# Forget logits with the tokens moving, two modulation pairs moved past a score bias, compressed products in another order

## The reference, cut to what matters

```python
# token mix of the first block: compressed attention, per head; 15 compressed keys
s_c = einsum('bghqd,bgnd->bghqn', qb, k_c) * scale - slope * d_c
p_c = masked_softmax(s_c, cmp_end <= t)
o_c = einsum('bghqn,bgnd->bghqd', p_c, v_c)

# hybrid layer
mod = silu(c) @ w_ada + b_ada              # 6 x 1024 values
h = modulate_2(x, norm1_w, shift1, scale1)
x_in, conv_b, conv_c, q, k, v, f_logit, gate_conv_l, gate_attn_l = split(h @ w_in)
log_f = log_sigmoid(f_logit + b_forget)    # 8 heads
F = cumsum(log_f)                          # along the tokens
s = q_i @ k.T * scale + (F_i[:, None] - F[None, :])
y_b = softmax(causal(s)) @ v               # q and k normed per head
merged = sigmoid(gate_conv_l) * p_a + sigmoid(gate_attn_l) * p_b
x = x + gate1 * (merged @ w_o)
```

## Time and profile before

| what | us |
|---|---|
| median of 3 runs | 1853.35 (1852.48 to 1854.16) |
| profiled execution, its own time | 1855.78 |
| its span, first to last instruction | 1854.1 |
| TensorE busy (matmul) in the span | 1764.3 (95%) |
| VectorE, ScalarE busy | 1376.3 (74%), 957.9 (52%) |
| mean granted TensorE clock, share of full | 0.978 |

### The profile page before, as it was taken

One profiled execution on the slowest core, in us unless ns is written; L12 is line 12 of the kernel. 1 busy time (PEld: TensorE's weight loads), 2 busy tenths in 40 slices (PEclk: granted clock), 3 DMA queues, 4 the chain that ended last, 5 costly groups with the idle time before them and its releaser, 6 DMA issues.

```text
span 1854.1 us, 24899 instructions
## 1 busy us (share of the span) xinstructions
PE 1764.3 (95%) x8645; PEld 1427.1 (77%) x8645; DVE 1376.3 (74%) x2097; ACT 957.9 (52%) x1433; POOL 46.9 (3%) x92
## 2 busy tenths in 40 slices
PE   5999999999999999999999999999899897999998
PEld 3788778787788878886878777887687775888876
DVE  6887676766876578777677578775776477999997
ACT  3444354664544454445437554444434546777775
POOL 0000000000000000000000000000000000000000
PEclk8999999999999999999989999999998998999999
DMA  8988743134576758884612338986562533999994
GB/s 361 359 324 301 287 172 136 69 127 169 204 280 257 255 187 336 316 305 174 248 69 92 135 138 311 343 302 245 189 253 93 203 136 114 363 347 375 347 350 166
DMA packets 61802, 437.43 MB, mean 236 GB/s; under 512 B 6816, under 2 KB 7328, under 8 KB 9504
## 3 DMA queue, kind: packets, MB, share of 16 engines
q1 hardware_dynamic: 47504, 339.27, 48.6%
q0 software_dynamic: 12672, 92.28, 13.4%
q10 hardware_dynamic: 1552, 4.89, 0.8%
HBM read 435.36 MB, written 1.05 MB: 235 GB/s over the span
## 4 chain that ended last, share of the span: by engine, by line
PE 82%; DVE 11%; ACT 4%; issue 2%; DMA 1%; ACTq 0%; SPq 0%; DVEq 0%; POOLq 0%
PE bank L1754 24%; PE bank L1755 24%; PE bank L1756 24%; DVE w_lo L945 2%; PE bank L1977 2%; DVE ada_w L969 1%; ACT w_hi L506 1%; PE bank L1995 1%; DMA ada_w<-ada_pairs 1%; PE bank L1836 1%; PE bank L1957 1%; DVE arena L1243 1%; PE bank L2005 1%; PE bank L1955 1%; PE bank L2297 1%
## 5 line engine op out<-in xcount | busy, mean ns | idle before, releaser
L945 DVE TENSOR_TENSOR w_lo<-raw,w_hi 128x1024 fp32r<-128x1024 f32 x426 | 501.5, 1220 | 223.2 <-ACT w_hi L506 222.9
L506 ACT ACTIVATE w_hi<-raw 128x1024 fp32r<-128x1024 f32 x426 | 426.5, 1053 | 363.3 <-PE bank L1756 359.2
L1754 PE MATMUL bank<-w_hi,uT_hi 128*128 128x512 f32 (+3 forms) x1424 | 558.4, 392 | 20.3 <-DVE uT_lo L1260 12.6
L1755 PE MATMUL bank<-w_lo,uT_hi 128*128 128x512 f32 (+3 forms) x1424 | 543.9, 382 | 0.0
L1756 PE MATMUL bank<-w_hi,uT_lo 128*128 128x512 f32 (+3 forms) x1424 | 543.4, 382 | 0.0
L1754 PEld LDWEIGHTS bank<-w_hi,uT_hi 128*128 128x128 f32 x1424 | 271.5, 191 | 80.1 <-DVE uT_lo L1260 14.0
L1756 PEld LDWEIGHTS bank<-w_hi,uT_lo 128*128 128x128 f32 x1424 | 270.7, 190 | 52.1
L1755 PEld LDWEIGHTS bank<-w_lo,uT_hi 128*128 128x128 f32 x1424 | 271.6, 191 | 48.6 <-issue 1.4
L1754 PE MATMUL bank<-w_hi,r_arena 128*128 128x512 f32 (+1 forms) x744 | 299.1, 402 | 6.2 <-DVE r_arena L1652 2.3
L1755 PE MATMUL bank<-w_lo,r_arena 128*128 128x512 f32 (+1 forms) x744 | 295.1, 397 | 0.0
L1756 PE MATMUL bank<-w_hi,r_arena 128*128 128x512 f32 (+1 forms) x744 | 292.6, 393 | 0.0
(11 more groups left out here) (328 smaller groups left out, 1470.6 us busy)
## 6 DMA issues: line engine op xcount, KB each, us to landing
raw<-weight_stream SPq DMA_DIRECT2D x216, 1024.0 KB, 4.9
ada_w<-ada_pairs POOLq DMA_DIRECT2D x88, 1024.0 KB, 5.2
raw<-expert_blocks SPq DMA_DIRECT2D x48, 1024.0 KB, 4.8
ada_w<-expert_blocks SPq DMA_DIRECT2D x32, 1024.0 KB, 4.9
cmpw<-expert_blocks SPq DMA_DIRECT2D x16, 1024.0 KB, 4.8
arena<-ada_pairs SPq DMA_DIRECT2D x5, 1024.0 KB, 13.8
ada_w<-ada_pairs SPq DMA_DIRECT2D x3, 1024.0 KB, 13.8
cmpw<-compress_w ACTq DMA_DIRECT2D x2, 1024.0 KB, 8.7
```

The costliest lines, as they stand in the source:

```text
L506: act.activation(w_hi[:, b], v, ACT.Copy).then_inc(hi_done, 1)
L945: V.tensor_tensor(w_lo[:, b], v, f32(w_hi[:, b]), ALU.subtract).then_inc(split_done, 1)
L1754: pe.matmul(dst, xh, w_hi[:, off:off + n], start=first, stop=False, skip_group_check=True)
L1755: pe.matmul(dst, xh, w_lo[:, off:off + n], start=False, stop=False, skip_group_check=True)
```

## The change

Three parts. The forget products hold 8 weight columns stationary and move 256 tokens, 24 products into 8 rows; ScalarE copies these to `f_lT`, TensorE turns them back between the two halves of gate set 0, and the copy to `f_row` waits for that. The last two of the late pairs leave the fourth unit; ScalarE copies `c_next` to `c_kept` (the second half of `cmpw`), and VectorE does the pairs from there, behind the first job's bias; VectorE's wait for all pairs ahead of the q and k norms goes. The compressed products run over the row groups in the innermost loop.

```diff
--- before.py
+++ after.py
@@ -218,6 +218,7 @@
         qkv = at(4096, T, HYB_QKV)
         gates_h = at(7168, T, 2 * D)
         gate_sets_h = [gates_h[:, :, i * 512:(i + 1) * 512] for i in range(4)]
+        f_lT = at(8704, T, P, parts=8)
         f_row = at(11264, T, 8)
         f_e, f_l, f_cum = at(11280, T, 8), at(11296, T, 8), at(11312, T, 8)
         nlogf = at(11392, T, P)
@@ -369,7 +370,8 @@
                 return (1, b + (13 + i // 2), g0 + (24 + i)) if i % 2 == 0 else (0, a + (13 + i // 2), g0 + (24 + i))
             return 1, b + (i + 13), g0 + (i + 26)
 
-        LATE_PAIRS = [(0, 1), (2, 3), (4, 5), (6, 7)]
+        LATE_PAIRS = [(0, 1), (2, 3), (4, 5), ()]
+        c_kept = cmpw[:, 1, 1024:2048]
 
         def late_pair(i):
 
@@ -778,10 +780,13 @@
                 split(u + m + 1, (2,))
 
             act.wait_ge(w_done, DEPTH * 7 + 5)
+            act.activation(f_lT[:, :, :], SPARE[0:8, 128:128 + S].rearrange("p (t s) -> p t s", t=T), ACT.Copy).then_inc(rT_ready, 1)
+            split(u + 5, (0,))
+            act.wait_ge(r_psum, 1)
             act.activation(f_row[:, :, :], SPARE[:, 0:16].rearrange("p (t h) -> p t h", t=T), ACT.Copy).then_inc(w_evac_a, 1)
-            split(u + 5, (0,))
             act.wait_ge(qkn_ms, 1)
             act.activation(qk_ss, qk_ss, ACT.Sqrt).then_inc(qkn_sq, 1)
+            act.activation(c_kept, c_next, ACT.Copy).then_inc(c_ready, 1)
 
             act.wait_ge(exp_in, 1)
             act.activation(f_e[:, :, :], f_e[:, :, :], ACT.Exp).then_inc(exp_out, 1)
@@ -796,6 +801,7 @@
                 act.wait_ge(q_psum, DEPTH * 2 + b + 1)
                 act.activation(qT_h[:, 2 * b:2 * b + 2], bank[2 + 4 * b][:, :].rearrange("p (c s) -> p c s", c=2), ACT.Copy,
                                scale=qk_gain[:, 0:1]).then_inc(q_ready, 1)
+            act.wait_ge(c_ready, 2 * DEPTH + 2)
             for b in range(2):
                 act.wait_ge(kh_psum, b + 1)
                 act.activation(kT_h[:, 2 * b:2 * b + 2], bank[4 + b][:, :].rearrange("p (c s) -> p c s", c=2), ACT.Copy,
@@ -1221,8 +1227,9 @@
                         e = V.tensor_tensor(ov[:, a], ov[:, a], tv[:, a], ALU.add)
                     link(e)
 
-            def jobs_run(j0, jobs, beside=lambda j: None):
+            def jobs_run(j0, jobs, beside=lambda j: None, first=lambda: None):
                 job_bias(j0, jobs, 0)
+                first()
                 for j, (kind, qt, g) in enumerate(jobs):
                     if j + 1 < len(jobs):
                         job_bias(j0, jobs, j + 1)
@@ -1500,7 +1507,6 @@
             link(V.tensor_tensor(f_row[:, :, :], f_row[:, :, :], bf, ALU.add))
             V.tensor_scalar(f_cum[:, :, :], f_row[:, :, :], 0.0, None, ALU.min)
             V.scalar_tensor_tensor(f_e[:, :, :], f_row[:, :, :], -1.0, f_row[:, :, :], ALU.mult, ALU.min).then_inc(exp_in, 1)
-            dve.wait_ge(ada_done, STAGES * PAIRS)
             dve.wait_ge(qkn_sq, 1)
             link(V.reciprocal(qk_ss, qk_ss))
             for i in range(2):
@@ -1552,7 +1558,12 @@
                 if j >= 2:
                     split(um, (j - 2,))
 
-            jobs_run(DEPTH * NJ, HYB_JOBS, hyb_beside)
+            def last_pairs():
+                dve.wait_ge(c_ready, 2 * DEPTH + 2)
+                for j in (6, 7):
+                    ada_pair(late_pair(j), mods[:, 72 + 2 * j:74 + 2 * j], c_kept)
+
+            jobs_run(DEPTH * NJ, HYB_JOBS, hyb_beside, first=last_pairs)
 
             def last_modulation():
                 dve.wait_ge(ada_done, STAGES * PAIRS)
@@ -1589,7 +1600,7 @@
                 V.tensor_tensor(xn_lo[:, t], xn[:, t], f32(xn_hi[:, t]), ALU.subtract).then_inc(xn_ready, 1)
             expert_split(0, 0, (0, 1), IN_LINE)
 
-            dve.wait_ge(r_psum, 1)
+            dve.wait_ge(r_psum, 2)
             link(V.tensor_copy(logits[:, :, :], GU[1][:, 128:256].rearrange("p (t c) -> p t c", t=T)[:, :, 0:36]))
             lg = logits[:, :, 0:4]
 
@@ -2106,10 +2117,10 @@
                 up(1, bank[3], 0, uk_psum)
                 up(0, bank[0], 1024, uv_psum)
                 pe.wait_ge(kvc_ready, l + 1)
-                for p in range(2):
-                    half = slice(DH * p, DH * p + DH)
-                    for qt in range(2):
-                        for i in range(4):
+                for qt in range(2):
+                    for i in range(4):
+                        for p in range(2):
+                            half = slice(DH * p, DH * p + DH)
                             m = pe.matmul(bank[4 + p][:, 64 * qt + 16 * i:64 * qt + 16 * i + N_CMP], qT[half, i, tok(qt)], kT_cmp[half, i // 2, 0:N_CMP],
                                           start=True, stop=True, skip_group_check=True)
                 m.then_inc(cs_psum, 1)
@@ -2129,10 +2140,10 @@
                     for i in range(2):
                         m = turn_rows(bank[Q_BANKS[b]][:, i * S:i * S + S], lambda t, h: q_tok[:, t, h], 2 * b + i, QK)
                     m.then_inc(qm_psum, 1)
-                for i in range(4):
-                    rows = slice(32 * i, 32 * i + N_CMP)
-                    for qt in range(2):
-                        for p in range(2):
+                for qt in range(2):
+                    for p in range(2):
+                        for i in range(4):
+                            rows = slice(32 * i, 32 * i + N_CMP)
                             m = pe.matmul(bank[CO_BANKS[i]][:, 128 * qt + 64 * p:128 * qt + 64 * p + 64], pT_cmp[rows, 2 * p + qt], v_cmp[rows, i // 2],
                                           start=True, stop=True, skip_group_check=True)
                 m.then_inc(co_psum, 1)
@@ -2193,8 +2204,9 @@
             seen = {m: set() for m in (4, 5, 6)}
             for k in range(KD):
                 need(u + 4, seen[4], 8 * k, 8)
-                for t in range(T):
-                    m = mm3(SPARE[:, 8 * t:8 * t + 8], uT_hi[:, k, tok(t)], uT_lo[:, k, tok(t)], 8 * k, 8, k == 0 and t == 0, k == KD - 1)
+                for w, v in ((w_hi, uT_hi), (w_lo, uT_hi), (w_hi, uT_lo)):
+                    m = pe.matmul(SPARE[0:8, 128:128 + S], w[:, 8 * k:8 * k + 8], v[:, k], start=k == 0 and w is w_hi and v is uT_hi,
+                                  stop=k == KD - 1 and v is uT_lo, skip_group_check=True)
             m.then_inc(used[0], 1)
             release(w_done)
 
@@ -2209,7 +2221,12 @@
 
             pe.wait_ge(w_evac_a, DEPTH * 9 + 6)
             pe.wait_ge(w_evac_v, DEPTH * 3 + 3)
-            hyb_gates(0)
+            hyb_gates(0, range(4))
+            pe.wait_ge(rT_ready, 1)
+            for t in range(T):
+                m = pe.transpose(SPARE[:, 8 * t:8 * t + 8], f_lT[:, t], ident[0:8, 0:8])
+            m.then_inc(r_psum, 1)
+            hyb_gates(0, range(4, KD))
             pe.wait_ge(logf_ready, 1)
             pe.matmul(SPARE[:, 0:8], tri[:, 0:P], nlogf[:, 0, 0:8], start=True, stop=True, skip_group_check=True)
             pe.matmul(SPARE[:, 8:16], ones, nlogf[:, 0, 0:8], start=True, stop=False, skip_group_check=True)
@@ -2276,7 +2293,7 @@
                                   stop=k == KD - 1 and v is uT_lo, skip_group_check=True)
             m.then_inc(rT_psum, 1)
             release(used[2])
-            pe.wait_ge(rT_ready, 1)
+            pe.wait_ge(rT_ready, 2)
             for t in range(T):
                 m = pe.transpose(GU[1][:, 128 + 64 * t:128 + 64 * t + 36], logits_T[:, t], ident[0:36, 0:36])
             m.then_inc(r_psum, 1)
```

## The result

The changed kernel takes 1840.82 us (median of 10 runs, 1836.00 to 1846.99). The kernel before, run beside it, takes 1852.25 (10 runs, 1848.82 to 1854.56). The ratio is 0.9942, with a 95% interval of 0.9931 to 0.9953: 11.4 us or 0.6% faster. The profiled execution of the changed kernel took 1841.11 us.

What follows compares the result with a forecast made beforehand. TensorE's own sequence and the handoffs it waits for were taken to bound the kernel. Hybrid stretch 3.4 plus layers 1.7 made 5.1 us off the 1853.35 median: 1848.2 us, range 1844.8 to 1851.6.

Steps and rivals of the forecast that it cites:

- The forget products: Hybrid layer: new products save 3.9 us, gate set 0 at full clock 1.9; TensorE reaches the sums 5.5 earlier.
- ScalarE as the next late thing: Hybrid layer: ScalarE's in-order chain delays q's copy, so the first scores come 4.1 us earlier, not 5.5.
- The pairs: Two late pairs, 4.6 us on VectorE, fit its later 9.34 us pause free; the hybrid gain needs their move.
- Queues: SP's expert loads, behind its stream, and POOL's pair loads are not delayed by the later pairs: nothing.
- The clock in the hybrid stretch: Clock falls with the first hybrid scores; 0.7 us lost, so the hybrid term is 4.1 - 0.7 = 3.4.
- Compressed products: Both layers' compressed attention: 0.0625 us per instruction, scores 2.0 (1.3 saved), sums 2.0 (0.5 saved).
- wide overlap rival: Compressed sums: alternated products run at 0.028 us each; 7.4 us saved in all, 1846.0; chance 0.16.
- The 0.8 for the first layer's scores: First layer: VectorE waited 0.78 us for the scores, so 0.8 of their saving counts on the path.
- Layers: Compressed attention in the first block's two layers: 0.5 us in the second plus 1.2 in the first, 1.7.
- No effect of alternation: Compressed products: each product's two passes keep one group, loads stay serial; 3.4 us alone, 1850.0; chance 0.12.
- drain at each change of group: Compressed products: 52 more row-group changes drain the array at 0.16 us each, 8.3 us; slower, 1858.2; chance 0.08.
- Clock: Hybrid layer: fall comes with the first scores, 3.4 us further into set 1; hybrid 0.9, total 2.6, 1850.7; chance 0.17.

Runs made afterwards that it cites:

- e5: Changed kernel with the two late pairs back in the fourth unit, VectorE's wait for them restored and the copy to c_kept gone: 1845.15 us, ratio 0.9954.
- e6: Changed kernel with the compressed sums taking turns over two row groups, not four: 1839.98 us, ratio 0.9929 against the kernel before.
- e10: The changed kernel run again, unchanged: 1842.73 us, ratio 0.9938 against the kernel before.
- e2: Changed kernel with both compressed loops in the old order (forget products and pairs alone): 1847.93 us, ratio 0.9972 against the kernel before.
- e8: Changed kernel plus seven zero products in TensorE's wait ahead of the first hybrid scores: 1839.31 us, ratio 0.9926 against the kernel before.
- e4: Kernel before with only the compressed sums in the new order: 1850.05 us, ratio 0.9980.
- e3: Kernel before with only the compressed scores in the new order: 1850.35 us, ratio 0.9980.
- e1: Kernel before with both compressed loops, scores and sums, in the new order: 1848.57 us, ratio 0.9971.
- e11: e1 run again, unchanged: 1846.40 us, ratio 0.9967 against the kernel before.

## Why the prediction was right in sign and wrong in size

**The forget products: right.** 3.9 saved was forecast and 3.9 came: from the product ahead of them to their release it was 7.65 us and is 3.74. Gate set 0 with the two turns in it takes 11.49 (1374.83 to 1386.32) where 10.9 + 0.26 was said, so the sums are reached 5.2 earlier and not 5.5. The window over all of it is at clock 1.00.

**ScalarE as the next late thing: right.** q was to be copied 3.4 us earlier and is 3.9 earlier, the first scores 4.1 and are 4.5. The chain waits where it was said to (3.51 for the turned f).

**The pairs: right.** They lie inside VectorE's pause and cost nothing, and e5 shows that the gain needs the move: 1.7 of the 4.5.

**Queues: right.** SP's expert loads still stand behind the stream, and moved with everything else.

**The clock in the hybrid stretch: 0.7 too dear in four of five profiles.** The fall was to come with the first scores, 8.1 us after the last gate product. In the profile it came 2.5 us into them, 9.9 after that product (2.6 to 3.2 into them in e5, e6 and e10); then the loss forecast doesn't arise, and the second scores keep the whole 4.5. e2's execution shows the other case, with a loss of 1.4 (41.86 against 40.45). On the Trainium skill's rule on transposes ("TensorE: Matmul & The Clock Gate", Part 4), by which turns keep nothing up: in e8, products of zeros between the turns and the scores remove the fall that follows the turns, which agrees with it; no run here took the turns themselves away.

**Compressed products: the scores right, the sums mis-sized.** 0.0625 an instruction was taken for all. The scores came to 1.96 (2.0 forecast), and became a longer wait in the second layer as forecast. The sums came to 1.12 (2.0 forecast), about 0.03 from start to start, which is the wide overlap rival's price: four groups in turn overlap further than the group boundary of the earlier trace rows showed, where two groups meet; e6 with two in turn has 1.61. The Trainium skill ("TensorE: Matmul & The Clock Gate", Part 3) has four row groups run about three times as fast as one; 2.60 to 1.12 is 2.3 times, so the direction agrees and the figure is not reached. With old sums and a full clock all through, the best rows of the sub-steps in these profiles give a layer of 5.33 + 2.35 + 2.33 + 7.00 + 5.85 = 22.86 (scores to turn, turn to sums, sums, to the gates, seven of these), and the new one is 21.34: 1.5 us a layer by the sums alone, 3.0 for both, where 1.0 was forecast. The 0.8 for the first layer's scores was not there: VectorE's wait of 0.78 stood in scores that were themselves partly at half clock (3.78 from first to last start, 3.06 in the second layer), so that row was a loss to the clock.

**Layers: the step that failed.** "Which may now fall elsewhere: 0.1 off" treated the half clock behind the layers' scores as something that stays and moves, and so put the clock at a small loss where it was the largest gain of that profile. It went from the layers, and a fall of 3.4 us came in behind the first of them (385.9, 1.6 us by the starts). The old layers are 25.51 and 26.42 where 22.86 is their length at full clock: 2.6 + 3.6 = 6.2 us were the clock's in that profile, and in the new order nearly none of it is left. Together with the sums' 3.0 that is the 9.25 measured, 1.7 forecast. The second layer's fall, the longer one (10.2 us from 953.0), was not read at all before the prediction, as only the first layer's window was. The medians give the parts too, each with an interval of 2 to 3 us to either side: the sums 3.1 (e4, half clock unchanged); the scores 2.8 (e3), which can only be the clock's, as the turn begins 5.28 us behind the first score in both of its layers, and 5.33 in the old order at full clock; the hybrid stretch 5.2 (e2). Together they are 11.1 of the 11.4, and the layers' share is 5.9, less than the one pair of profiles shows.

**How much of it is the whole kernel's.** Over all runs the half clock fell from 83.9 to 64.1 us, 20 less. Among 35 runs of the kernel before, measured together, an execution is 0.38 us longer for each us of half clock; at that rate 20 us are 7.5 of the 11.4 us. The two profiles, in which it fell from 81.9 to 67.6, say where: the falls of 6.8 in the forget products and of 6.8 and 10.2 in the layers are gone, which is 23.8, and 3.4 in the start-up; in came 3.4 each at 385.9 and 853.5, 3.4 more at 1293.8 and 2.7 at the end of the kernel. e4 is the control: its half clock is unchanged, and it gains only the 3.1 of its shorter sums. The forecast had the hybrid's share of this (gates at full clock) and nothing for the layers'.

**The rivals.** Wide overlap: right for the sums, too small as a whole (7.4). No effect of alternation and drain at each change of group: refuted, the products are shorter in every profile in the new order. Clock: it went the other way, except in single executions such as e2's.

**What stays open.** What in the old order brings the clock down is not settled. It goes with the order of the scores (e3 against e4), and it isn't idle time alone: e3 leaves TensorE idle longer ahead of the turn and has less half clock. Which of the scores' length, their loads or their spacing counts, no run here tells apart. Nor is it settled why e1's layers, shorter by 9.2 in its profile, come to 4.6 and 7.2 by medians; its mean half clock (74.3, and 58.9 in the profile) says that its other executions fall more often, e11's profile shows one such fall in the first layer, and where the rest lie no profile shows.

## What to carry to other kernels

Where small products use only some of the rows, let neighbouring instructions take different row groups, as many in turn as there are, and price them by a row in which as many groups take turns. When such a stretch shows a granted clock of 0.50, read that window in every place where the stretch occurs, and put the whole of its half clock into the range as a gain that may come: here another order of the small products took most of the falls away. A fall that was lifted by products of zeros was worth 3.1 us in its stretch (e8) and nothing that showed in the median, so such an edit is judged by the median and the mean clock of many runs, not by its stretch.

## What the runs showed of the hardware that was not expected

- The fp32 sums of 15 rows take, for 32 instructions, 2.60 us with eight in one row group in a row, 1.61 with two groups in turn and 1.12 with four.
- TensorE is busy for 23.69 of the 26.42 us of the second layer in the old order and has a mean granted clock of 0.81; in the new order it is busy for 17.11 of 21.34, and has 1.00. More idle time (4.23 against 2.73 us) went with a higher clock.
- The same kernel's half clock differs from one execution to the next (83.9 us in the mean of 35, standard deviation 7.3), with the same instructions throughout, and the times follow it at 0.38 us per us.
- 24 products with 8 stationary columns and 256 moving take 2.7 us at clock 1.00; the 48 with 128 stationary and 8 moving took 6.7, and the clock fell to 0.50 while they ran.
